# Expert weights: gate and up of most experts in one 4 MB transfer, in a ring of ten adjacent places

## The chip, the cores and the metric

The kernel runs on one core of a Trainium2 chip. Its time is the device time of one execution in microseconds, as the median of three runs. Two layers are computed, and each has an expert phase in which all 32 experts' weights are read from HBM, whatever the tokens are.

## What is computed

Two layers of a decoder with 512 tokens of width 1024, all in float32. A layer is a token mixer (a short gated convolution in layer 0, a chunked mLSTM in layer 1) beside a cross-attention into a memory, an output projection, a LayerNorm, a mixture of 32 experts, and a second LayerNorm. The change touches the experts alone:

```python
def expert_block(args):
    xblk, e = args
    h = jax.nn.silu(xblk @ w_gate[e]) * (xblk @ w_up[e])
    return h @ w_down[e]
```

`w_gate` and `w_up` are 1024 x 512, `w_down` is 512 x 1024 for each expert: three matrices of 2 MB. A token goes to two experts of one group of four, so that an expert has some 32 tokens.

## The kernel before

**The stream of weights.** The host packs the weights of a layer into `w_pack[l, e, 3, 128, 4096]`, a unit being `[128, 4096]` floats, 2 MB in one piece of HBM with 16 KB for each partition. Units 0 and 1 of an expert are gate and up together, each for half of the 1024 input rows (`("gu", e, 0)`, `("gu", e, 1)`); the third is down (`("dn", e, 0)`). `STREAM` (lines 42 to 45) lists a layer's 96 units in the order of their loads: both halves of expert 0, then for each expert e its two gate-and-up halves and the down unit of expert e - 1, and last the down unit of expert 31.

**The ring.** Ten places of 16 KB in each partition hold units: nine in the tensor `ring`, and the tenth, place 9, in the tensor `xT`, which stands behind `x_sb` (lines 96 to 99; `unit`, line 162). Unit n goes to place `PLACE[n % 10]` (line 50), so it takes the place of unit n - 10. The same memory serves the other phases: `R0`, `R1` and `R2` are thirds of the ring, and several split weights and activations of the mLSTM phase lie at fixed places of it.

**Who issues and who waits.** SP issues all loads, on one queue, in stream order. Units 0 to 9 are issued in the output projection ahead of the expert phase (`out_sp`, lines 702 to 717). Units 10 and 11 go in halves, each half when TensorE has read that half of the place (`half_read`, lines 1158 to 1162). Units 12 to 93 go whole: `unit_free(n - UNITS)` waits until TensorE is through with the old unit, then `load_unit` issues the transfer (lines 1163 to 1165). A gate-and-up unit is free at `gu_done`, a down unit at `y_done`. Units 94 and 95 go in two halves each (lines 1166 to 1171). In layer 0, loads for the mLSTM phase follow on the same queue, each behind `vacated(place)`.

TensorE waits for a unit with `unit_landed` (line 185), one semaphore for each place. For expert e it does the two halves of gate and up (`gate_up`, line 1235, matmuls at line 1244), the gather of later rows (line 1230), `combine` of expert e - 2 (line 1311), `down` of expert e - 1 (line 1282, matmuls at line 1294) and small transposes. `gate_up` asks for its two halves one after the other; `down` asks for its unit alone.

GpSimd gathers and scatters the tokens' rows through its own queue, 512 KB each, eight of each kind in a layer.

Of the kernel before, what the change touches and what calls it, by code (L numbers as in the profile page):

```python
# [4 lines left out]
F32 = mybir.dt.float32  # L5
# [8 lines left out]
P = 128  # L14
D_MODEL = 1024
SEQ = 512
DEPTH = 2
# [9 lines left out]
N_EXPERTS = 32  # L27
# [7 lines left out]
KT = D_MODEL // P  # L35
MT = MEM_LEN // P
BLK = 64
RING = 3
W_UNIT = 4096
W_EXP = 3 * W_UNIT  # L40
UNITS = 3 * RING + 1
STREAM = [("gu", 0, 0), ("gu", 0, 1)]
for _e in range(1, N_EXPERTS):
    STREAM += [("gu", _e, 0), ("gu", _e, 1), ("dn", _e - 1, 0)]
STREAM += [("dn", N_EXPERTS - 1, 0)]
SLOTS = 128
BIG = 1e30
SMALLS = 352
GATE_ROWS = 96 + ML_HEADS
PLACE = (0, 1, 2, 5, 4, 6, 8, 7, 3, 9)  # L50
EARLY = (0, 0)
HALVED = 2


class Chain:
# [16 lines left out]
def build_trunk(nc, x, xT_in, memT_in, conv_slabs, conv_qm, mlstm_w_in, smalls, w_kv_mem, w_out,  # L72
                ln1_g, ln1_b, ln2_g, ln2_b, w_pack, out):
    ctx = ExitStack()
    with ctx:
        phase_sems = []

        def sb(name, shape, dt=F32, at=ctx):
            return at.enter_context(nc.sbuf_tensor(name, shape, dt))

        def sem(name, at=ctx):
            if at is ctx:
                return ctx.enter_context(nc.semaphore(name))
            handle = nc.alloc_semaphore(name=name)
            phase_sems.append(handle)
            return handle
# [6 lines left out]


        ring_at = -(-nc.sbuf_base // 32) * 32
        ring = sb("ring", [P, RING * W_EXP])
        x_sb = sb("x_sb", [P, TT, D_MODEL])
        xT_at = -(-nc.sbuf_base // 32) * 32
        xT = sb("xT", [P, KT, SEQ])
        ident = sb("ident", [P, P])  # L100
        future_big = sb("future_big", [P, P])
        before = sb("before", [P, P], BF16)
# [52 lines left out]
        in_unit = [None] * DEPTH  # L155

        def place_of(kind, e, h=0):

            n = STREAM.index((kind, e, h))
            return PLACE[n % UNITS], n // UNITS  # L160

        def unit(i):
            if i == 3 * RING:
                return xT[:, :, :].rearrange("p k s -> p (k s)")
            return ring[:, i * W_UNIT:(i + 1) * W_UNIT]

        def gate_up_view(i):
            return unit(i).rearrange("p (c f x) -> p c f x", c=4, f=2)

        def down_view(i):  # L170
            return unit(i).rearrange("p (f c d) -> p f c d", f=2, c=2)

        def load_unit(eng, l, n):

            kind, e, h = STREAM[n]
            at = PLACE[n % UNITS]
            eng.dma_start(unit(at), w_pack[l, e, 2 if kind == "dn" else h]).then_inc(in_unit[l][at], 16)

        def load_half(eng, l, n, a):

            kind, e, h = STREAM[n]
            at, z = PLACE[n % UNITS], slice(W_UNIT // 2 * a, W_UNIT // 2 * (a + 1))
            eng.dma_start(unit(at)[:, z], w_pack[l, e, 2 if kind == "dn" else h][:, z]).then_inc(in_unit[l][at], 16)

        def unit_landed(eng, l, kind, e, h=0):

            i, use = place_of(kind, e, h)
            by_halves = use and i in PLACE[:HALVED]
            eng.wait_ge(in_unit[l][i], 16 * (use + (2 if by_halves else 1)))

# [884 lines left out]
        def load_mlstm_slab(sp, i):  # L1077
            c, w = slabs[i]
            sp.dma_start(R0[:, (i % 2) * 4096:(i % 2) * 4096 + KT * w], mlstm_w_in[:, KT * c:KT * (c + w)]
                         ).then_inc(in_w[i % 2], 16)  # L1080

        def expert_phase(l, mem_l):
# [3 lines left out]
            with ph:  # L1086
                s = lambda n: sem(f"{n}_{l}", ph)
# [26 lines left out]
                half_read = s("p2_half_read")  # L1114
                in_unit[l] = [s(f"in_unit_{i}") for i in range(UNITS)]
                back = [s(f"p3_back{t}") for t in range(TT)]
# [21 lines left out]
                with nc.Block() as block:  # L1138
                    @block.sync
                    def _(sp):  # L1140
                        def unit_free(n):

                            kind, e, h = STREAM[n]
                            if kind == "gu":
                                sp.wait_ge(gu_done, 2 * e + h + 1)
                            else:
                                sp.wait_ge(y_done, e + 1)

                        def vacated(place):

                            unit_free(max(n for n in range(len(STREAM)) if PLACE[n % UNITS] == place))

                        if l == 0:
                            conv_sp(sp)
                        out_sp(sp)
                        for row, dst in ((ln2_g, ln_g), (ln2_b, ln_b)):
                            sp.dma_start(dst[0:1, :], row[l].unsqueeze(0)).then_inc(in_ln, 16)
                        for n in range(UNITS, UNITS + HALVED):
                            sp.wait_ge(half_read, n - UNITS + 1)
                            load_half(sp, l, n, 0)  # L1160
                            unit_free(n - UNITS)
                            load_half(sp, l, n, 1)
                        for n in range(UNITS + HALVED, len(STREAM) - 2):
                            unit_free(n - UNITS)
                            load_unit(sp, l, n)
                        for i, e in enumerate((LAST - 1, LAST)):
                            at, _ = place_of("dn", e)
                            unit_free(len(STREAM) - 2 + i - UNITS)
                            for f, done in ((0, in_unit[l][at]), (1, last_dn[i])):
                                sp.dma_start(down_view(at)[:, f], w_pack[l, e, 2].rearrange("p (f c d) -> p f c d", f=2, c=2)[:, f]  # L1170
                                             ).then_inc(done, 16)
                        if not last_layer:
                            vacated(7)
                            sp.dma_start(wkv[:, 0], w_kv_mem[1].rearrange("p (h k n) -> p h k n", h=2, k=KT)[:, 0]
                                         ).then_inc(in_kv_half[0], 16)
                            sp.wait_ge(gu_done, 2 * N_EXPERTS)
                            sp.dma_start(memT, memT_in.rearrange("p (k m) -> p k m", k=KT)).then_inc(in_mem2, 16)
                            sp.dma_start(wkv[:, 1], w_kv_mem[1].rearrange("p (h k n) -> p h k n", h=2, k=KT)[:, 1]
                                         ).then_inc(in_kv_half[1], 16)
                            vacated(0)  # L1180
                            load_mlstm_slab(sp, 0)
                        later_sp(sp)
                        for i in range(3):
                            sp.wait_ge(scattered[i], 16 * len(range(i, N_GROUPS, 3)))
                        if not last_layer:
                            for t in range(TT):
                                sp.dma_start(x_sb[:, t, :], x2_dram[t * P:(t + 1) * P, :]).then_inc(back[t], 16)
                            vacated(1)
                            load_mlstm_slab(sp, 1)
# [29 lines left out]
                    def _(pe):  # L1219
# [15 lines left out]
                        def gate_up(e, halves=(0, 1)):  # L1235
                            if e >= 2:
                                pe.wait_ge(hid_done, e - 1)
                            for h in halves:
# [3 lines left out]
                                for c in range(4):  # L1242
                                    for f in range(2):
                                        last = nc.tensor.matmul(GU_BANK[e % 2][64 * f:64 * f + 64, :],  # L1244
                                                                xgT[e // 2 % 2][:, 4 * h + c, 64 * (e % 2):64 * (e % 2) + 64],
                                                                gu[:, c, f, :], start=(h == 0 and c == 0), stop=(h == 1 and c == 3))
                                    if c == 1 and 2 * e + h < HALVED:
                                        last.then_inc(half_read, 1)
# [327 lines left out]
        def later_blocks(l, ph, x1_rows, to_rows, ln_g, ln_b, scattered, acc_read):  # L1576
# [4 lines left out]
            s = lambda n: sem(f"later_{n}_{l}", ph)  # L1581
# [41 lines left out]
            def later_sp(sp):  # L1623
                def before():
                    for i in range(3):
                        sp.wait_ge(scattered[i], 16 * len(range(i, N_GROUPS, 3)))
                    for t in range(TT):
                        sp.dma_start(x_sb[:, t, :], x1_rows[t * P:(t + 1) * P, :]).then_inc(again, 16)

                def step(e, n, b):  # L1630
                    sp.wait_ge(y_done, n + 1)
                    for h, done in ((0, in_gu1), (1, in_gu1), (2, in_dn1)):
                        sp.dma_start(unit(3 + h), w_pack[l, bass.ds(e, 1), h].rearrange("o p x -> p (o x)")).then_inc(done, 16)

                def after():
                    for t in range(TT):
                        sp.wait_ge(normed, t + 1)
                        sp.dma_start(to_rows[t * P:(t + 1) * P, :], x_sb[:, t, :]).then_inc(put, 16)
                    sp.wait_ge(put, 16 * TT)
                turns(sp, step, before=before, after=after)  # L1640
# [906 lines left out]
```

## Time and profile before

| | us |
|---|---|
| median of three runs | 1393.65 (1392.25 to 1394.54) |
| span of the profiled execution | 1392.8 |
| TensorE busy in it | 1338.4 (96%) |
| layer 0, expert units from first issue to last half | 142 to 652 |
| layer 1, the same | 874 to 1378 |
| HBM read | 460 MB |

The profile is one execution, so its span stands beside the median of the runs and not for it. Times within it count from the span's start. Matmuls overlap, so that TensorE's busy share is high whether it waits or not. A DMA issue is known by the time at which SP issued it, and by the microseconds from there to its landing; the packets of a queue are counted with their bytes and the share of the 16 DMA engines' time that they took. "DMA share" in a stretch is that of all queues and can come out a little over 1, as packets overlap. The transfers to place 9 have the name `xT` and the others `ring`.

### The profile page before, as it was taken

To read this page: it belongs to the slowest core of one execution; us is meant where nothing else is said; L and a number is where in the kernel's file an instruction comes from. 1 tells how busy PE (TensorE), PEld (TensorE's weight loads), DVE (VectorE), ACT (ScalarE), POOL (GpSimd) and SP (SyncE) were. 2 spreads that over 40 slices of the span, in tenths; PEclk is the share of its full clock that TensorE was granted. 3 is DMA by queue.
4 is the path that set the end of the run, shared out by engine and by line. 5 is a ranking of instruction groups with operands and counts; after the bars stand their busy time and mean duration, and the time that the engine had idled before them with its cause. 6 is when DMAs were issued, how large, how long until landed. Compare 5 with 4: busy or idle time off the path is not lost. (4 is left out here: it accounts for less than half of the span.)

```text
span 1392.8 us, 16438 instructions
## 1 busy us (share of the span) xinstructions
PE 1338.4 (96%) x6694; PEld 711.7 (51%) x6694; DVE 509.8 (37%) x1038; ACT 306.1 (22%) x534; POOL 41.4 (3%) x66
## 2 busy tenths in 40 slices
PE   8999999999999999989899999999999999999896
PEld 7878783333333333333787788774333333333332
DVE  5366583122122121222554358782132122122122
ACT  5242341011011010111443236441011011010111
POOL 1000000000000000000000000000000000000000
PEclk9999999999999999999999999999999999999998
DMA  9420879999999999999431201989999999999995
GB/s 376 172 92 0 363 293 372 427 426 428 427 425 427 427 428 426 427 428 392 190 121 61 106 16 61 409 335 382 429 428 426 428 426 428 428 425 428 427 427 225
DMA packets 41395, 465.36 MB, mean 334 GB/s; under 512 B 6602, under 2 KB 6754, under 8 KB 13030
## 3 DMA queue, kind: packets, MB, share of 16 engines
q1 hardware_dynamic: 36422, 454.83, 78.4%
q0 software_dynamic: 4608, 8.40, 1.6%
q8 instruction: 55, 0.90, 0.3%
q10 hardware_dynamic: 288, 1.05, 0.2%
q14 instruction: 22, 0.18, 0.0%
HBM read 460.05 MB, written 12.60 MB: 339 GB/s over the span
## 5 line engine op out<-in xcount | busy, mean ns | idle before, releaser
L1244 PE MATMUL bank<-ring,kv_sb 128*64 128x512 f32 x960 | 214.7, 596 | 11.2 <-DMA ring<-in_w_pack 11.1
L1244 PE MATMUL bank<-ring,onehot 128*64 128x512 f32 x896 | 203.7, 603 | 13.4 <-DMA ring<-in_w_pack 13.4
L1294 PE MATMUL bank<-ring,pad 128*64 128x512 f32 x928 | 211.8, 598 | 1.8 <-issue 1.1
L1244 PEld LDWEIGHTS bank<-ring,kv_sb 128*64 128x64 f32 x960 | 68.4, 137 | 135.8 <-issue 135.5
L1294 PEld LDWEIGHTS bank<-ring,pad 128*64 128x64 f32 x928 | 61.8, 136 | 143.8 <-issue 135.0
L1244 PEld LDWEIGHTS bank<-ring,onehot 128*64 128x64 f32 x896 | 64.4, 138 | 131.7 <-issue 131.7
L1407 ACT ACTIVATE pad<-bank 128x256 f32<-128x256 f32 x64 | 24.5, 383 | 437.1 <-PE bank L1244 437.1
L1413 ACT COPY pad<-bank 128x512 f32<-128x512 f32 x64 | 37.4, 585 | 329.2 <-PE bank L1294 329.2
L1497 DVE COPY onehot<-bank 128x512 f32<-128x512 f32 x32 | 22.1, 691 | 237.0 <-PE bank L1230 237.0
L1507 DVE COPY pad<-bank 128x256 f32<-128x256 f32 x64 | 27.0, 422 | 173.5 <-PE bank L1269 173.5
L1497 DVE COPY kv_sb<-bank 128x512 f32<-128x512 f32 x28 | 19.4, 691 | 188.8 <-PE bank L1230 188.8
L1230 PEld LDWEIGHTS bank<-x_sb 128*128 128x128 f32 x480 | 58.1, 191 | 48.6 <-issue 47.1
L1311 PE MATMUL bank<-pad,x_sb 64*128 64x512 f32 x256 | 71.7, 639 | 0.0
L1230 PE MATMUL bank<-x_sb 128*128 128x128 f32 x480 | 69.5, 288 | 0.0
L497 PE MATMUL bank<-x_half_hi,w_half_hi 128*128 128x512 f32 x160 | 63.0, 394 | 1.5 <-DVE x_half_lo L577 1.1
L497 PE MATMUL bank<-x_half_lo,w_half_hi 128*128 128x512 f32 x160 | 62.3, 389 | 0.0
L497 PE MATMUL bank<-x_half_hi,w_half_lo 128*128 128x512 f32 x160 | 62.3, 389 | 0.0
L1975 PE MATMUL bank<-x_half_hi,w_half_hi 128*128 128x512 f32 x112 | 44.0, 393 | 0.0
L1975 PE MATMUL bank<-x_half_hi,w_half_lo 128*128 128x512 f32 x112 | 43.6, 390 | 0.0
L1975 PE MATMUL bank<-x_half_lo,w_half_hi 128*128 128x512 f32 x112 | 43.6, 389 | 0.0
L2106 DVE TENSOR_TENSOR w_half_lo<-ring,w_half_hi 128x1024 fp32r<-128x1024 f32 x24 | 29.5, 1239 | 37.5 <-ACT w_half_hi L2066 37.5
L1501 DVE TENSOR_TENSOR pad<-pad,bank 128x256 f32<-128x256 f32 x64 | 26.3, 410 | 30.0 <-ACT pad L1407 30.0
(345 smaller groups left out, 1723.4 us busy)
## 6 DMA issues: line engine op xcount, KB each, us to landing
ring<-in_w_pack SPq DMA_DIRECT2D x166, 2048.0 KB, 27.3
xT<-in_w_pack SPq DMA_DIRECT2D x18, 2048.0 KB, 30.1
ring<-in_w_pack SPq DMA_DIRECT2D x16, 1024.0 KB, 25.1
ring<-in_mlstm_w_in SPq DMA_DIRECT2D x6, 2048.0 KB, 8.4
ring<-in_conv_slabs SPq DMA_DIRECT2D x5, 1536.0 KB, 12.1
ring<-in_w_out SPq DMA_DIRECT2D x1, 4096.0 KB, 13.8
x_rows<-x_sb SPq DMA_DIRECT2D x6, 512.0 KB, 8.2
ring<-in_xT SPq DMA_DIRECT2D x4, 512.0 KB, 6.7
```

The costliest lines, as they stand in the source:

```text
L497: last = nc.tensor.matmul(o[:, :], w[:, k, :], xh[:, k, :], start=(k == 0 and w is w_hi and xh is x_hi), stop=(k == KT - 1 and w is w_lo))
L1230: last = nc.tensor.matmul(o[:, c * P:(c + 1) * P], xg[g % 3][:, 512 * h + c * P:512 * h + (c + 1) * P], pick[g % 2][:, 2 * (q % 2):2 * (q ...
L1244: last = nc.tensor.matmul(GU_BANK[e % 2][64 * f:64 * f + 64, :], xgT[e // 2 % 2][:, 4 * h + c, 64 * (e % 2):64 * (e % 2) + 64], gu[:, c, f ...
L1294: last = nc.tensor.matmul(Y_BANK[e % 2][64 * n:64 * n + 64, :], hidT[e % 2][:, c, 64 * f:64 * f + 64], dn[:, f, c, 512 * n:512 * n + 512], ...
L1311: last = nc.tensor.matmul(ACC[n][:, :], gateT[e // 2 % 2][rows, e % 2, :], y[e % 2][rows, :], start=(j == 0), stop=(j == PER_GROUP - 1))
L1407: nc.scalar.activation(hid[e % 2][:, :], GU_BANK[e % 2][:, 0:256], ACT.Silu).then_inc(activated, 1)
L1413: nc.scalar.copy(y[e % 2][:, :], Y_BANK[e % 2][:, :]).then_inc(y_copied, 1)
L1497: V.tensor_copy(xgT[q % 2][:, 4 * h:4 * h + 4, :], o[:, :].rearrange("p (c r) -> p c r", c=4)).then_inc(xcopied, 1)
L1501: V.tensor_tensor(hid[e % 2][:, :], hid[e % 2][:, :], GU_BANK[e % 2][:, 256:512], ALU.mult).then_inc(hid_done, 1)
L1507: V.tensor_copy(hidT[e % 2][:, :, :].rearrange("p c r -> p (c r)"), H_BANK[:, 0:256]).then_inc(hcopied, 1)
L1975: last = nc.tensor.matmul(o[:, :], w[:, k, :], xh[:, k, :], start=(k == 0 and w is hi and xh is x_hi), stop=(k == KT - 1 and w is lo))
L2106: last = V.tensor_tensor(of(lo), part, of(hi), ALU.subtract)
```

## The change

Ten places now lie in one tensor `ring`, place 9 behind place 8; `xT` is laid over place 9, and `x_sb` comes after. The first ten units keep their old places (`FIRST_PLACES`). Later units go round the ring in the order 0, 1, 2, 4, 5, 6, 7, 8, 9, 3 (`PLACES`), and each waits for the last unit that had its place, which is no longer always unit n - 10. `PAIRED` lists the first gate-and-up units from 14 on whose second half goes to the next place; expert 31 is left out. That gives 19 pairs in a layer: experts 5 to 9, 12, 14 to 19, 22 and 24 to 29. A pair is one transfer of 4 MB (`load_pair`), issued when both places are free, with one semaphore increment, and both of its halves wait for that (`landing`). The host packs the weights as `w_pack[l, e, 128, 3, 4096]`, so that a partition's three units lie one behind the other, 48 KB in all: a pair is a run of 32 KB for each partition, a single unit a run of 16 KB with 48 KB from one partition's to the next. Matmuls and their order stay.

```diff
-PLACE = (0, 1, 2, 5, 4, 6, 8, 7, 3, 9)
+FIRST_PLACES = (0, 1, 2, 5, 4, 6, 8, 7, 3, 9)
+PLACES = (0, 1, 2, 4, 5, 6, 7, 8, 9, 3)
+PLACE = FIRST_PLACES + PLACES * (-(-len(STREAM) // UNITS) - 1)
+PAIRED = [n for n in range(14, len(STREAM) - 4) if STREAM[n][0] == "gu" and STREAM[n][2] == 0 and PLACE[n + 1] == PLACE[n] + 1]
+
+
+def landing(n):
+
+    first = n - 1 if n - 1 in PAIRED else n
+    at = PLACE[first]
+    counts = [16 * (2 if UNITS <= m < UNITS + HALVED else 1) for m in range(first + 1) if PLACE[m] == at and m - 1 not in PAIRED]
+    return at, sum(counts)
...
-        ring = sb("ring", [P, RING * W_EXP])
+        ring = sb("ring", [P, UNITS * W_UNIT])
+        xT_at = ring_at + 4 * RING * W_EXP
+        xT = nc.alloc_sbuf_tensor_at("xT", [P, KT, SEQ], F32, offset=xT_at)
+        units = ring[:, :].rearrange("p (i x) -> p i x", x=W_UNIT)
         x_sb = sb("x_sb", [P, TT, D_MODEL])
-        xT_at = -(-nc.sbuf_base // 32) * 32
-        xT = sb("xT", [P, KT, SEQ])
...
-            at = PLACE[n % UNITS]
-            eng.dma_start(unit(at), w_pack[l, e, 2 if kind == "dn" else h]).then_inc(in_unit[l][at], 16)
+            at = PLACE[n]
+            eng.dma_start(unit(at), w_pack[l, e, :, 2 if kind == "dn" else h]).then_inc(in_unit[l][at], 16)
+
+        def load_pair(eng, l, n):
+
+            _, e, _ = STREAM[n]
+            at = PLACE[n]
+            eng.dma_start(units[:, at:at + 2, :], w_pack[l, e, :, 0:2]).then_inc(in_unit[l][at], 16)
...
-            i, use = place_of(kind, e, h)
-            by_halves = use and i in PLACE[:HALVED]
-            eng.wait_ge(in_unit[l][i], 16 * (use + (2 if by_halves else 1)))
+            at, count = landing(place_of(kind, e, h)[1])
+            eng.wait_ge(in_unit[l][at], count)
...
+                        def place_free(n):
+
+                            unit_free(max(m for m in range(n) if PLACE[m] == PLACE[n]))
...
                         for n in range(UNITS + HALVED, len(STREAM) - 2):
-                            unit_free(n - UNITS)
-                            load_unit(sp, l, n)
+                            if n - 1 in PAIRED:
+                                continue
+                            place_free(n)
+                            if n in PAIRED:
+                                place_free(n + 1)
+                                load_pair(sp, l, n)
+                            else:
+                                load_unit(sp, l, n)
...
-    pack = _np.empty((DEPTH, N_EXPERTS, 3, P, W_UNIT), _np.float32)
+    pack = _np.empty((DEPTH, N_EXPERTS, P, 3, W_UNIT), _np.float32)
```

## Rows read from the trace of the kernel before

**Rows 1.** The page, 40 slices: share of the DMA engines, rate.
```profile
DMA  9420879999999999999431201989999999999995
GB/s 376 172 92 0 363 293 372 427 426 428 427 425 427 427 428 426 427 428 392 190 121 61 106 16 61 409 335 382 429 428 426 428 426 428 428 425 428 427 427 225
```
**Rows 2.** Stretches of layer 1's expert phase: engines, clock, DMA share, GB/s.
```profile
936.00:991.00 55.00, 55.00 (x310) 21.33 (x310) 14.46 (x38) 7.53 (x14) 3.11 (x3) 0.97 0.97 390
...
1050.00:1200.00 150.00, 150.00 (x718) 55.15 (x716) 37.81 (x73) 19.61 (x32) 6.04 (x6) 1.00 1.01 427
```
**Rows 3.** Chain of waits, two experts' beginnings: start us, us, what.
```profile
991.00 7.02 PE bank L1244 x32
...
1004.12 7.02 PE bank L1244 x32
```
**Rows 4.** Chain of waits, the end of layer 1.
```profile
1215.42 43.36 DMA ring<-in_w_pack
...
1262.60 45.70 DMA ring<-in_w_pack
...
1317.86 44.86 DMA ring<-in_w_pack
```
**Rows 5.** Groups by line: busy, mean ns, then idle us before and releaser.
```profile
L1244 PE MATMUL bank<-ring,kv_sb 128*64 128x512 f32 x960 | 214.7, 596 | 11.2 <-DMA ring<-in_w_pack 11.1
...
L1244 PE MATMUL bank<-ring,onehot 128*64 128x512 f32 x896 | 203.7, 603 | 13.4 <-DMA ring<-in_w_pack 13.4
...
L1244 PE MATMUL bank<-xT,onehot 128*64 128x512 f32 x128 | 29.1, 596 | 2.5 <-DMA xT<-in_w_pack 2.5
```
**Rows 6.** Waits of SP's queue: us in total, times, longest.
```profile
SPq L177 <- PE bank L1244: 400.5, 110, 9.7
SPq L177 <- PE bank L1294: 287.1, 54, 6.3
```
**Rows 7.** SP's timeline, one issue each: start us, us of issuing.
```profile
241.26 0.33 SPq L177 DMA_DIRECT2D ring<-in_w_pack  x1
257.81 0.33 SPq L177 DMA_DIRECT2D xT<-in_w_pack  x1
...
958.09 0.33 SPq L177 DMA_DIRECT2D ring<-in_w_pack  x1
968.18 0.33 SPq L177 DMA_DIRECT2D ring<-in_w_pack  x1
977.34 0.33 SPq L177 DMA_DIRECT2D ring<-in_w_pack  x1
984.72 0.33 SPq L177 DMA_DIRECT2D xT<-in_w_pack  x1
994.63 0.33 SPq L177 DMA_DIRECT2D ring<-in_w_pack  x1
```
**Rows 8.** us to landing of those issued at 241.26, 257.81, 968.18, 984.72, 994.63; w_out.
```profile
ring<-in_w_pack SPq DMA_DIRECT2D x1, 2048.0 KB, 8.3
xT<-in_w_pack SPq DMA_DIRECT2D x1, 2048.0 KB, 12.0
ring<-in_w_pack SPq DMA_DIRECT2D x1, 2048.0 KB, 8.7
xT<-in_w_pack SPq DMA_DIRECT2D x1, 2048.0 KB, 11.8
ring<-in_w_pack SPq DMA_DIRECT2D x1, 2048.0 KB, 11.7
...
ring<-in_w_out SPq DMA_DIRECT2D x1, 4096.0 KB, 13.8
```
**Rows 9.** SP's queue from 56.61 to 63.87, then 276 to 299: packets, MB, share.
```profile
q1 hardware_dynamic: 95, 3.11, 99.2%
...
q1 hardware_dynamic: 677, 9.78, 100.1%
```
**Rows 10.** SP's queue from 779 to 784.5, an mLSTM slab landing: packets, MB, share.
```profile
q1 hardware_dynamic: 129, 1.82, 77.7%
```

## What the change should do to the time

> **What bounds the kernel now.** Both expert phases stream 96 units of 2 MB per layer, and the question is whether TensorE or the stream sets their end. I read the 40-slice view first [rows 1]: in both expert phases the DMA row stands at 9 and the GB/s row at 425 to 428 from a slice after the start to the end. The stretches [rows 2] say it more finely: in the first 55 us of layer 1's phase the 16 DMA engines are 0.97 busy at 390 GB/s, then 1.01 at 427, up to the end. So DMA idles only near the start of the phase, and from then on never. PE does one expert in 13.1 us (two beginnings of gate and up, 991.00 and 1004.12 [rows 3]); three units at 428 GB/s are 3 x 2.097 MB / 428 = 14.7 us. PE is the faster of the two by 1.6 us per expert, and it begins with a full ring of ten units (49 us of stream). That lead is used up after some 25 experts. The chain of waits [rows 4] ends so: its last 170 us hold three pieces "DMA ring<-in_w_pack" of 43 to 46 us, with some matmuls between them. A transfer that takes 44.9 us from issue to landing with 4.9 us of own work has nine others ahead of it: the queue is full and PE waits for it. By lines, gate and up lost 11.1 + 13.4 + 2.5 = 27.0 us to w_pack transfers in the two phases [rows 5]. So the time is: when the last unit lands, plus a tail that does not change. And the last unit lands when the first did, plus 4.9 us per unit, plus **every microsecond in which the DMA queue ran dry**. It can run dry only early, while PE frees places slowly and the ring is full; SP itself waits for PE 400.5 + 287.1 us before such transfers [rows 6], which costs nothing while older transfers are queued.
>
> **Part 1: what a pair waits for (the dear part).** A transfer is issued when its place is free; from the issue times I read when each place is freed. In the kernel before, unit n takes the place of unit n-10, so the issue time of unit n is the time at which unit n-10 was used up. After the change, the places of the first ten units keep the old order (0, 1, 2, 5, 4, 6, 8, 7, 3, 9) and the later ones run 0, 1, 2, 4, 5, 6, 7, 8, 9, 3. So unit 13 now needs the place of unit 4 (before: 3), the pair 14+15 those of 3 and 5, unit 16 that of 7 (before: 6), the pair 17+18 those of 6 and 9, unit 19 that of 8, the pair 20+21 those of 10 and 11. In layer 1 units 4, 5, 7, 9 and 11 are used up at 958.09, 968.18, 977.34, 984.72 and 994.63 [rows 7]. PE does not move in this stretch: it reads units that landed long ago.
> Two prices are needed. A 2 MB unit issued into an empty queue lands after 8.7 us (issued at 968.18) or 8.3 us (issued at 241.26) [rows 8]; 8.5 less its own 4.9 leaves 3.6 us of way. A 4 MB transfer into an empty queue thus takes 8.5 + 4.8 = 13.1 to 13.3 us; the one that the trace has, w_out, took 13.8 [rows 8]. I take 13.1 (it is nearest in kind) and keep 13.8 for the range. Behind other transfers a unit lands 4.9, a pair 9.7 us after the one ahead.
> Layer 1, landing by landing. Unit 13: issued at 958.09, where before unit 14 stood; 958.1 + 8.5 = 966.6. Pair 14+15: issued at 968.18, lands at 968.2 + 13.1 = 981.3 (unit 15 landed at 968.2 + 8.7 = 976.9 before). Unit 16: issued at 977.34, 981.3 + 4.9 = 986.2. Pair 17+18: issued at 984.72, 997.8. Unit 19: 1002.7, where before it landed at 984.72 + 11.8 = 996.5 [rows 8]. Pair 20+21: 1002.7 + 9.7 = 1012.4, where before unit 21 landed at 994.63 + 11.7 = 1006.3 [rows 8]. **The stream is 6.1 us late.** From here the queue does not run dry: the next pair could land alone 13.1 us after its issue, which follows 13.1 us behind the last pair's, and the queue ahead of it needs 14.6.
> Layer 0 with its own times [rows 7]: pair 14+15 issued at 241.26, lands at 254.4; unit 16 at 259.3; pair 17+18 issued at 257.81, lands at 270.9; unit 19 at 275.8, before 257.81 + 12.0 = 269.8 [rows 8]: 6.0 late, 5.8 after the pair 20+21.
>
> **Part 2: what 32 KB runs save.** 19 pairs per layer fit the condition (experts 5 to 9, 12, 14 to 19, 22, 24 to 29; the others fall on the steps from place 2 to 4, 9 to 3 or 3 to 0, and expert 31 is left out), 16 of them after unit 21. The trace has 32 KB packets in one place, w_out: 95 packets in a window of 7.26 us at a share of 99.2%, so 0.992 x 16 x 7.26 / 95 = 1.213 us each. For weights in 16 KB packets: 9.78 MB in a window of 23 us are 597 of them (the other 80 are four bytes each), 1.001 x 16 x 23 / 597 = 0.617 us [rows 9]. Two small ones 1.23, one large 1.213: 0.02 us per large packet, eight of them per engine and pair, 0.16 us. But the weights in that window shared the engines with a few packets of other queues and w_out did not, so I take 0.10 and get 16 x 0.10 = 1.6 us per layer. The bound below is 0 (two packets of 16 KB are sent after all), above 0.2. This is small because a queued transfer here shows no fixed cost that could be merged away.
> The Trainium skill says otherwise: "DMA: Bandwidth & Descriptors", section "Anatomy of one DMA", gives each DMA a fixed cost of about 2 us beside its bytes, and the section "Rules for kernel authors" asks for large transfers. As an estimate by that page, 38 transfers less would give 76 us; the trace disagrees for queued transfers, since 2 MB at 428 GB/s leave none of the 2 us.
>
> **Part 3: the HBM layout.** A unit was 2 MB in one piece; now a partition's three units lie together, so an unpaired unit is 128 runs of 16 KB at a pitch of 48 KB. The nearest row is the mLSTM slab: 16 KB runs at a pitch of 107 KB; in a window of 5.5 us 1.82 MB, or 111 packets, took 0.777 x 16 x 5.5 / 111 = 0.616 us each [rows 10], the price of the contiguous weights. I take 0; for the range 0.5% of the stream either way, 2 us per layer, since that row is of a queue with one transfer only.
>
> **Part 4: what lies on no path.** SP issues 19 transfers less per layer, while it waits for PE anyway [rows 6]. Late in the phase PE waits for a pair's second half before it starts the first: 4.9 us at expert 29, which it wins back over the unpaired experts 30 and 31: after the landing of pair 29 PE has three times 13.1 us [rows 3] and a tail of 2 us to do, some 41.3 us; the stream has eight units of 4.9 us and a half unit's matmuls of 1.8 us behind the last, some 41.1. So 0.2 us per layer, 0.4 in all. If that cover were gone the price would be up to 4.9 us per layer. Gathers and scatters share the engines with packets that are twice as long: eight turns of 0.6 us more, and their rows are wanted tens of us later. xT's move behind the ring changes no instruction. The last units before the mLSTM phase keep their places' order to within one unit.
>
> **Sum.** Layer 1: +6.1 - 1.6 + 0.2 = +4.7. Layer 0: +5.8 - 1.6 + 0.2 = +4.4. Both carry to the end one for one, since the stream sets both ends. +9.1 us. The profiled execution (span 1392.8) would become 1401.9; the median of the runs is 0.85 above that span, so 1393.65 + 9.1 = **1402.7 us**.
>
> **The rivals.** (a) *The two runs are not merged* into one packet, or 32 KB packets cost the same per byte: Part 2 gives 0, the delay stands: 1393.65 + 6.1 + 5.8 + 0.4 = 1406. For it: only w_out shows such packets. Against: it does show them. (b) *The 48 KB pitch costs* in the full stream: 1% of some 390 us per layer is 3.9, 1402.7 + 7.8 = 1410. Against: rows 10. (c) *Not slower: the full stream runs faster*, by larger packets or by another spread over HBM. The price to beat is 4.5 us in 75 units, 0.06 us of 4.9 per unit, in paired and unpaired ones alike; it decides from 433 GB/s where rows 2 have 427, and gives 1394 there. Only the pairs have a reason for it, and at 1.213 us per packet they reach 432; gathers and scatters, which take the rest, stay. (d) *Each transfer has a fixed cost that the merge saves*: were it of the size of the way, 3.6 us for each of 38 transfers, the stream would stop being the bound, and PE's 27.0 us of waits are all that there is to win, 1367. Against: rows 9, where queued transfers keep the engines at 100.1%. (The Trainium skill's section on the fixed cost, named in Part 2, stands for this rival.)
>
> **How the numbers follow.** Forecast 0.68 (1399.5 to 1405.5: savings of 0 to 0.2 per pair, ways of 13.1 to 13.8); (a) 0.08; (b) 0.10; (c) 0.10, of which 0.08 ends within 0.2% (2.8 us, about what a measurement can tell) and 0.02 faster; (d) 0.04. Slower 0.86, same 0.08, faster 0.06. The range goes from 1397.5, the forecast with 0.5% less for the layout, to 1408, which holds (a) and the lower half of (b).
>
> **What would show it.** In the profile after: GB/s in the first 55 us of each expert phase below 390 and the DMA share below 0.97; the issue of unit 13 at 958, of the pairs at 968 and 985; after that a rate of 428 to 430; more than 27.0 us of PE's waits for w_pack, nearer 37, and beginning some four experts earlier; the mLSTM phase some 4 us later. The forecast is wrong if the share early in the phase is not lower, or if the full stream runs above 433 or below 425 GB/s.

## The result and the profile after

The changed kernel takes 1408.53 us as the median of four runs (1406.30 to 1409.45), beside 1394.10 us for the kernel before in the same session. The ratio on record, which is not the quotient of these two medians (1.0103), is 1.0101, with a 95% interval of 1.0085 to 1.0116. That is 14.1 us slower, between 11.9 and 16.2. A second session with the same kernel gave 1.0091 (1.0075 to 1.0108), 12.7 us. The forecast was 1402.7 us, with a range up to 1408.0: the direction was right, the size was not.

The profiled execution has a span of 1407.0 us. Four views of it answer rows of before.

First the page's 40 slices, as [rows 1]. What is new stands where an expert phase begins, in slices 7 and 28 to 29: 335, and 353 and 394 GB/s, where before it was 372, and 382 and 429.

```profile
DMA  9420978999999999998431202989999999999994
GB/s 374 169 91 0 379 293 335 407 424 434 427 425 435 422 429 431 428 428 360 188 120 61 105 16 78 407 333 353 394 428 433 424 433 430 422 430 430 427 428 199
```

Then stretches, as [rows 2]: us, busy time of PE, PEld, DVE, ACT and POOL, granted share of the clock, DMA share, GB/s. The first 55 us of layer 0's and of layer 1's expert phase, the same stretch of the full stream as before, and 17 us at the start of the mLSTM phase; then, from the kernel before, the 55 us of layer 0 that [rows 2] lack.

```profile
209.40:264.40 55.00, 55.00 (x316) 21.57 (x317) 15.12 (x40) 7.66 (x14) 3.20 (x3) 1.00 0.90 352
943.60:998.60 55.00, 55.00 (x316) 21.54 (x316) 15.29 (x40) 7.64 (x14) 3.12 (x3) 1.00 0.90 347
...
1050.00:1200.00 150.00, 145.53 (x692) 54.39 (x691) 37.56 (x73) 19.23 (x31) 5.03 (x5) 1.00 1.01 429
674.00:691.00 17.00, 13.12 (x95) 10.97 (x94) 7.78 (x10) 8.05 (x12) 2.26 (x4) 0.90 0.58 228
```

```profile
209.00:264.00 55.00, 55.00 (x309) 21.35 (x307) 14.62 (x38) 7.58 (x14) 3.33 (x3) 0.97 0.97 392
```

Where the DMA share was 0.97 before it is 0.90 now, in both layers; afterwards the engines are full as before, and this stretch runs at 429 GB/s in place of 427. So the loss is dry time at the start, as forecast; what the full stream gained is read from its landings below.

SP's issues at the start of layer 1, as [rows 7]: unit 13, the pair 14+15, unit 16, the pair 17+18 and unit 19; below, in the same order, the sizes and us to landing, as [rows 8].

```profile
965.75 0.33 SPq L187 DMA_DIRECT2D ring<-in_w_pack  x1
974.26 0.33 SPq L193 DMA_DIRECT2D ring<-in_w_pack  x1
983.37 0.33 SPq L187 DMA_DIRECT2D ring<-in_w_pack  x1
990.80 0.33 SPq L193 DMA_DIRECT2D ring<-in_w_pack  x1
991.17 0.43 SPq L187 DMA_DIRECT2D ring<-in_w_pack  x1
```

```profile
ring<-in_w_pack SPq DMA_DIRECT2D x1, 2048.0 KB, 7.5
ring<-in_w_pack SPq DMA_DIRECT2D x1, 4096.0 KB, 13.4
ring<-in_w_pack SPq DMA_DIRECT2D x1, 2048.0 KB, 9.4
ring<-in_w_pack SPq DMA_DIRECT2D x1, 4096.0 KB, 14.8
ring<-in_w_pack SPq DMA_DIRECT2D x1, 2048.0 KB, 19.3
```

The transfers wait for what the prediction named: unit 19 lands at 991.2 + 19.3 = 1010.5. Layer 1's stream began 7.6 us later than before (its first load was issued at 881.9, not 874.3), so that 1010.5 - 7.6 - 996.5 = 6.4 us were lost since. In layer 0, with no such shift, the pair 20+21 lands at 266.5 + 18.9 = 285.4, and unit 21 did at 279.6: 5.8 us.

The chain of waits at its end, as [rows 4] (start us, us, what):

```profile
1119.63 37.24 DMA ring<-in_w_pack
...
1160.74 40.43 DMA ring<-in_w_pack
...
1205.03 40.81 DMA ring<-in_w_pack
...
1312.65 38.87 DMA ring<-in_w_pack
```

and the two groups of gate and up, as [rows 5]:

```profile
L1269 PE MATMUL bank<-ring,onehot 128*64 128x512 f32 x1024 | 234.0, 610 | 17.1 <-DMA ring<-in_w_pack 17.1
...
L1269 PE MATMUL bank<-ring,kv_sb 128*64 128x512 f32 x1024 | 231.6, 605 | 17.2 <-DMA ring<-in_w_pack 17.2
```

TensorE waits 34.3 us for weights, not 27.0, and the chain's first transfer now stands at 1120 us instead of 1215. The later part of the phase is set by the stream more than before.

The 14.2 us between the two profiled executions split by milestones, each an issue or a landing of the traces, so:

| stretch | layer 0 | layer 1 |
|---|---|---|
| up to the landing of unit 9 | -0.2 | -0.1 |
| unit 9 to unit 21 landed | +6.0 (66.1 to 72.0) | +6.4 (66.7 to 73.1) |
| unit 21 to the last half landed | -0.8 (371.7 to 370.9) | -0.1 (371.2 to 371.1) |
| last landing to layer 1's first issue, or to the end | +2.6 (222.9 to 225.6) | +0.3 |

### The profile page after: what moved, and what is told of

Read it like the earlier page. It is cut to its first block and busy times, and to the rows that moved or that the text cites. A ratio compares the mean times of both kernels' runs of the same rounds, so it can differ in the third digit from the quotient of the medians.

```text
span 1407.0 us, 16438 instructions
## 1 busy us (share of the span) xinstructions
PE 1344.2 (96%) x6694; PEld 718.1 (51%) x6694; DVE 510.0 (36%) x1038; ACT 306.3 (22%) x534; POOL 41.2 (3%) x66
## 5 line engine op out<-in xcount | busy, mean ns | idle before, releaser
L1269 PE MATMUL bank<-ring,onehot 128*64 128x512 f32 x1024 | 234.0, 610 | 17.1 <-DMA ring<-in_w_pack 17.1
L1269 PE MATMUL bank<-ring,kv_sb 128*64 128x512 f32 x1024 | 231.6, 605 | 17.2 <-DMA ring<-in_w_pack 17.2
L1319 PE MATMUL bank<-ring,pad 128*64 128x512 f32 x1024 | 233.7, 598 | 1.1 <-issue 1.1
L1269 PEld LDWEIGHTS bank<-ring,kv_sb 128*64 128x64 f32 x1024 | 76.6, 139 | 149.8 <-issue 149.5
L1269 PEld LDWEIGHTS bank<-ring,onehot 128*64 128x64 f32 x1024 | 75.4, 140 | 152.0 <-issue 152.0
L1319 PEld LDWEIGHTS bank<-ring,pad 128*64 128x64 f32 x1024 | 68.4, 136 | 157.5 <-issue 156.1
L512 PEld LDWEIGHTS bank<-x_half_hi,w_half_hi 128*128 128x128 f32 x160 | 30.0, 188 | 10.7 <-DVE w_half_lo L581 2.0
```

The costliest lines, as they stand in the source:

```text
L512: last = nc.tensor.matmul(o[:, :], w[:, k, :], xh[:, k, :], start=(k == 0 and w is w_hi and xh is x_hi), stop=(k == KT - 1 and w is w_lo))
L1319: last = nc.tensor.matmul(Y_BANK[e % 2][64 * n:64 * n + 64, :], hidT[e % 2][:, c, 64 * f:64 * f + 64], dn[:, f, c, 512 * n:512 * n + 512], ...
```

## The experiments

The theory, called the queue theory in the expectations, is that of the forecast: the time is the dry time of the DMA queue at the start of each phase, less a little for each pair. Its rivals were that the pairs cost something of their own, that the layout in HBM does, and that the late pairs lower TensorE's clock at a price. Ratios are against the kernel before in the same session, and the us beside them are the ratio's. "First 55 us" are the 55 us that begin 2.2 to 2.4 us before SP issues unit 10, as in [rows 2] and in the stretches above. A mean clock is the granted share of the clock over the span, as the median of a kernel's runs.

**The order of places without pairs.**

```diff
-PAIRED = [n for n in range(14, len(STREAM) - 4) if STREAM[n][0] == "gu" and STREAM[n][2] == 0 and PLACE[n + 1] == PLACE[n] + 1]
+PAIRED = []
```

> The changed kernel without pairs: the new order of places and the new layout of the weights stay, every unit is a transfer of its own. Queue theory (the time is the dry time of the DMA queue early in the phase): unit 13 still waits for the down unit of expert 0 and unit 18 for the second half of expert 3, so the order alone costs about 4.3 us per layer, 8.7 in all: 1394.1 + 8.7 = 1402.8, with the DMA share of the first 55 us between before and after. Rival (what costs is that a pair waits for two places): without pairs the time falls back to 1394. If the pairs also lower the clock late in the phases, the mean granted clock here is 0.995 as before, not 0.987.

1.0045 (1.0031 to 1.0059), +6.3 us, between 4.3 and 8.2, where 8.7 were expected; median 1401.77. The rival falls: with no pair at all more than a third of the loss remains. It lies at the start of the phases:

```profile
209.10:264.10 55.00, 55.00 (x317) 21.59 (x317) 15.14 (x40) 7.69 (x14) 3.19 (x3) 1.00 0.93 370
937.30:992.30 55.00, 55.00 (x316) 21.48 (x316) 15.21 (x40) 7.58 (x14) 3.12 (x3) 1.00 0.93 371
```

The price per layer was put a little too high (4.3; the interval reaches to 4.1). Unit 9 to 21 took 69.9 and 68.6 us. The mean clock was 0.994 to 0.995, as without the change.

**Pairs only where the queue is full.**

```diff
-PLACE = FIRST_PLACES + PLACES * (-(-len(STREAM) // UNITS) - 1)
-PAIRED = [n for n in range(14, len(STREAM) - 4) if ...]
+PLACE = FIRST_PLACES * 4 + PLACES * (-(-len(STREAM) // UNITS) - 4)
+PAIRED = [n for n in range(40, len(STREAM) - 4) if ...]
```

> The changed kernel with the old order of places for the first 40 units and the new one, with 13 pairs per layer, from unit 40 on, where four transfers are queued. Queue theory: no dry time early, 13 pairs save 0.10 us each: 1.25 per layer, 1394.1 - 2.5 = 1391.6. Clock theory (late pairs make TensorE stand still longer, the granted clock falls to half in stretches, one of them at the start of the mLSTM phase): 2 to 3 us on top, 1394, and a mean clock below 0.99. Rival (pairs cost something of their own in the full queue): 1397 or more.

0.9998 (0.9987 to 1.0008), no difference: between -1.8 and +1.1 us. The loss is gone, with 13 pairs per layer in place, so pairs in a full queue have no price that this run shows; but the 2.5 us that they should save are not there either. The mean clock was 0.988. In the profile layer 1's first 55 us are not dry (in layer 0 they have 387 GB/s at 0.97):

```profile
934.60:989.60 55.00, 55.00 (x316) 21.50 (x316) 15.25 (x40) 7.63 (x14) 3.12 (x3) 1.00 0.99 399
```

**The layout in HBM alone**, on the kernel before:

```diff
-            eng.dma_start(unit(at), w_pack[l, e, 2 if kind == "dn" else h]).then_inc(in_unit[l][at], 16)
+            eng.dma_start(unit(at), w_pack[l, e, :, 2 if kind == "dn" else h]).then_inc(in_unit[l][at], 16)
...
-    pack = _np.empty((DEPTH, N_EXPERTS, 3, P, W_UNIT), _np.float32)
+    pack = _np.empty((DEPTH, N_EXPERTS, P, 3, W_UNIT), _np.float32)
```

> The kernel before with the new layout of the weights in HBM alone (a partition's three units one behind the other, 16 KB runs at a pitch of 48 KB). If the layout costs nothing, 1394.1 within 1 us and 16 KB packets of 0.615 us on average in the full stream; if it is what is missing in the forecast (5 us), 1399, and packets of 0.62 us or more.

1.0000 (0.9991 to 1.0010), median 1396.00 beside 1394.64. From unit 21 to the last half it takes 371.5 and 371.1 us, before 371.7 and 371.2, and its 16 KB packets in the full stream take 0.615 us on average. A pitch of 48 KB has no cost clear of the noise, which is 1.4 us.

**Pairs up to expert 19.**

```diff
-PAIRED = [n for n in range(14, len(STREAM) - 4) if ...]
+PAIRED = [n for n in range(14, 60) if ...]
```

> The changed kernel with pairs up to expert 19 alone (12 per layer instead of 19). Queue theory: the early dry time stays, 7 savings of 0.10 us per layer are lost: 1408.5 + 1.4 = 1409.9. Clock theory: without late pairs TensorE's waits are short as before, no half clock late in the phases and at the start of the mLSTM phase, 2 to 3 us less than that: about 1407, with a mean clock of 0.993 or more.

1.0085 (1.0071 to 1.0100), +11.9 us, between 9.9 and 13.9; median 1408.32 beside 1394.64. By the ratio 1409.9 lies too high and 1407 within, while the median itself lies between the two: whether the late half clock has a price, this run does not tell. The mean clock returned to 0.995, so the half clock late in the phases comes with the late pairs. Unit 9 to 21 took 76.2 and 75.7 us, with 336 and 338 GB/s in the first 55 us at a clock of 0.97.

**Waiting for both halves, without pairs**, on the kernel before:

```diff
                             for h in halves:
                                 pe.wait_ge(xcopied, h + 1 if e == 0 else 2 * (e // 2) + 2)
+                                if h == 0 and 12 <= e < LAST - 1:
+                                    unit_landed(pe, l, "gu", e, 1)
                                 unit_landed(pe, l, "gu", e, h)
```

> The kernel before, in which TensorE waits for both halves of gate and up before it begins the first one, for experts 12 to 29; transfers, places and layout are those of before. Queue theory: the stream does not change, TensorE wins the 4.9 us of a bunched wait back over experts 30 and 31: 1394.6 + 0.4 = 1395.0. Clock theory (the bunched waits lower the granted clock): mean clock 0.991 or less, half clock in stretches after 460 and after 1220 us, as in the changed kernel; if these have a price of their own, 2 to 3 us more, 1397.5.

0.9991 (0.9982 to 1.0000), median 1393.49. The bunched waits of Part 4 cost nothing that can be measured. The clock was 0.992 on average over the runs (0.990 to 0.994), lower than before's 0.995, but not as low as with late pairs: bunched waits are at most a part of what lowers it.

**The changed kernel once more.** No edit.

> The changed kernel once more, for a second profile. Queue theory: from the landing of unit 9 to that of unit 21 it takes 72 to 76 us per layer, against 66 to 67 before, whatever the clock does; 1408.5. If the half clock at the start of the mLSTM phase belongs to the change, the time from layer 0's last landing to layer 1's first issue is again 225 us or more, and not 222 to 223.

1.0091 (1.0075 to 1.0108), median 1406.76. This profiled execution was the fastest of its six runs, with a span of 1402.2 us. Unit 9 to 21 took 75.3 and 70.9 us, the second a little below the 72 to 76 expected. The time from layer 0's last landing to layer 1's first issue was 222.2 us, as before: the extra 2.6 us at the start of the mLSTM phase do not come with the change each time. The first two stretches are the starts of the phases, the third the 17 us that lost clock in the first profile (0.90 there, 1.00 here):

```profile
208.20:263.20 55.00, 55.00 (x309) 21.43 (x307) 14.46 (x38) 7.47 (x14) 3.19 (x3) 0.97 0.87 339
940.80:995.80 55.00, 55.00 (x316) 21.52 (x316) 15.28 (x40) 7.62 (x14) 3.08 (x3) 1.00 0.90 354
...
674.00:691.00 17.00, 14.75 (x110) 12.25 (x109) 10.15 (x14) 7.87 (x12) 2.27 (x4) 1.00 0.74 291
```

**Pairs in the middle alone.**

```diff
+PLACE = FIRST_PLACES * 3 + PLACES * (-(-len(STREAM) // UNITS) - 3)
+PAIRED = [n for n in range(30, 68) if ...]
```

> The changed kernel with the old order of places for the first 30 units and 8 pairs per layer, from unit 35 to 66: the queue is full at the first of them, and the last lie before TensorE begins to wait for the stream. Queue theory: 0.10 us saved per pair, 0.8 per layer: 1394.6 - 1.6 = 1393.0, mean clock 0.995 as before. If pairs cost something in a full queue, 1395 or more; if late pairs alone do, less than e2_late_pairs had (1394.75).

0.9998 (0.9987 to 1.0009). Again no difference; the 1.6 us that 16 pairs should have saved lie within the interval, so this run neither shows nor excludes them. The mean clock, 0.990, was lower than expected although the last pair is that of unit 65.

**The same waits, two transfers instead of one.** Units of a pair are issued one behind the other when both places are free.

```diff
-                            if n in PAIRED:
+                            if n in TOGETHER:
                                 place_free(n + 1)
-                                load_pair(sp, l, n)
-                            else:
-                                load_unit(sp, l, n)
+                            load_unit(sp, l, n)
```

(`TOGETHER` is the changed kernel's `PAIRED`, and `PAIRED` is empty.)

> The changed kernel, in which each pair is issued as two transfers of 2 MB, one behind the other, when both places are free: its waits and places stay, the merged transfer goes. Queue theory as forecast: the early dry time stays at about 6 us per layer, since two units on an empty queue land 8.5 + 4.9 = 13.4 us after the issue, and the saving of the runs is lost: 1394.7 + 12.6 = 1407.3. If the excess over the forecast is the way of a 4 MB transfer on an empty queue (the second pair took 13.5 to 15.5 us in the profiles so far), the pair 17+18 lands 13.4 us after its issue here, and unit 9 to 21 takes 72.5 us or less per layer. Rival (the merge itself costs): the time falls to 1400 or less.

1.0095 (1.0078 to 1.0111), +13.3 us where 12.6 were expected, median 1408.44. With no merged transfer the loss is the same within the noise. So the waits for places are the loss, and the merge is not. SP's two issues for units 17 and 18 at 990.54, which landed after 10.3 us as the mean of the two, the first after 7.5 and so the second after 13.1:

```profile
990.54 0.80 SPq L188 DMA_DIRECT2D ring<-in_w_pack  x2
...
ring<-in_w_pack SPq DMA_DIRECT2D x2, 2048.0 KB, 10.3
```

The second was issued 0.37 us behind the first, so from the first issue to the last landing it took 13.5 us, and 13.3 in layer 0. The same pair merged took 12.9 and 14.8 in the profile after, and 12.9 to 15.5 (14.5 on average) in the six phases of the three profiles that have it: some 1 us more, which the whole times do not show. Unit 9 to 21 took 71.6 and 72.9 us, and unit 21 to the end 371.7 and 371.9, without the saving. The starts of the phases:

```profile
208.40:263.40 55.00, 55.00 (x309) 21.37 (x307) 14.44 (x38) 7.48 (x14) 3.20 (x3) 0.97 0.87 339
941.70:996.70 55.00, 55.00 (x308) 21.25 (x306) 14.53 (x38) 7.53 (x14) 3.13 (x3) 0.97 0.88 343
```

**All pairs but the first two.**

```diff
-PAIRED = [n for n in range(14, len(STREAM) - 4) if ...]
+PAIRED = [n for n in range(20, len(STREAM) - 4) if ...]
```

> The changed kernel without its first two pairs (units 14+15 and 17+18 go one by one), 17 pairs per layer stay. Queue theory: the early loss is that of the order of places alone, as in e1_order_only (2.7 us per layer in its profile), less 0.05 to 0.1 us for each of 17 pairs: 1394.7 + 2 x (2.7 - 1.3) = 1397.5, up to 1400 by the landing-by-landing sum. Rival (later pairs cost as much as the first two): 1406 or more.

1.0032 (1.0022 to 1.0042), +4.5 us, between 3.1 and 5.9; median 1399.97, at the upper of the two times expected. Two pairs per layer of 19 carry some two thirds of the loss in the measured times: with them it is 12.7 to 14.1 us. The rival falls. The starts of the phases:

```profile
209.10:264.10 55.00, 55.00 (x309) 21.39 (x307) 14.44 (x38) 7.47 (x14) 3.19 (x3) 0.97 0.90 359
939.10:994.10 55.00, 55.00 (x309) 21.34 (x309) 14.37 (x39) 7.53 (x14) 3.25 (x3) 0.97 0.91 361
```

**The old order for one round more.**

```diff
-PLACE = FIRST_PLACES + PLACES * (-(-len(STREAM) // UNITS) - 1)
-PAIRED = [n for n in range(14, len(STREAM) - 4) if ...]
+PLACE = FIRST_PLACES * 2 + PLACES * (-(-len(STREAM) // UNITS) - 2)
+PAIRED = [n for n in range(20, len(STREAM) - 4) if ...]
```

> The changed kernel with the old order of places for the first 20 units, and 17 pairs per layer from unit 20 on. Queue theory: nothing of the first round is left to wait longer; the pair 20+21 meets a queue of little depth: +0.4 us per layer, 1394.7 + 0.7 = 1395.4, unit 9 to 21 in 67 us per layer. Rival (pairs or the adjacent ring cost something besides the first ten replacements): 1399 or more.

1.0002 (0.9993 to 1.0012), median 1395.14. With 17 pairs per layer in the adjacent ring the loss is gone from the measured time, when the first ten replacements alone keep the old order. What the change costs in that time comes with units 10 to 19. The starts of the phases are again those of before:

```profile
209.20:264.20 55.00, 55.00 (x309) 21.37 (x307) 14.45 (x38) 7.52 (x14) 3.19 (x3) 0.97 0.97 388
939.20:994.20 55.00, 55.00 (x310) 21.27 (x308) 14.45 (x38) 7.47 (x14) 3.12 (x3) 0.97 0.97 386
```

Behind them this profile has a loss of its own: unit 9 to 21 took 69.9 and 70.2 us, not the 67 expected. The pair 20+21 waits for the place of unit 11 and landed 12.3 and 10.9 us behind unit 19, where units 20 and 21 took 9.8 before. The next 20 us have 373 and 394 GB/s, before 426 and 428, which is 2.5 and 1.6 us of stream. The execution took 1399.16 us, the longest of twelve and 4.0 above their median; how much of this a usual execution has, no trace shows.

No variant was clearly faster than the kernel before; the nearest is the wait for both halves, at 0.9991 with an interval that ends at 1.0000.

## Why the prediction was right or wrong

**What bounds the kernel: right.** The same stretches in all profiles put the loss where the DMA queue ran dry, and nowhere else of the same size.

**Part 1, what a pair waits for: right in its mechanism and nearly in its size.** It said 5.8 and 6.1 us per layer; the first profile has 6.0 and 6.4. Some of that closeness is luck: the issue times came from an execution with 3.4 us at half clock early in each phase, the first profile had none there, so that the pairs were issued 1.2 to 1.5 us earlier than forecast, and in layer 1 the second pair took 1.7 us longer. A fairer size comes from GB/s at the same clock, since the start of a phase has in some executions 3.4 us at half clock, 1.2 instead of 2.4 GHz (0.97 in the rows), and in others none (1.00). At 0.97 the old order of places has 392 and 390 before, 388 and 386 in the last experiment, 389 on average, the changed waits 339 [the second profile], 339 and 343 [two transfers], 340 on average. That is 49 x 55 / 428 = 6.3 us of stream per layer. At 1.00: 399 [pairs where the queue is full, layer 1] against 352, 347 and 354, 351 on average, 6.2 us. The profiles whose rows are not shown fit: 387 to 389 at 0.97 and 395 to 401 at 1.00 with the old order. The order alone is 399 less 370.5 at 1.00, 3.7 us, and the kernel without the first two pairs gives the same at 0.97 (389 less 360); the prediction did not split it off, and the expectation of the first experiment put it at 4.3. The other 2.5 us are the first two pairs, 5 in both layers; the measured times give them 8 to 10, and this difference stays open.
One price in it was too low for the second pair: 13.1 us for 4 MB on an empty queue. The first pair took 12.4 to 13.4 us in the three profiles that have it, the second one, which finds the end of unit 16 still on the way, 12.9 to 15.5. I had kept w_out's 13.8 as the upper bound; four of these six lie beyond it.
The 8.5 us for 2 MB were misread in one point: the queue was not empty at these issues. The transfer ahead of the one issued at 968.18 landed at 969.95, that of 241.26 at 242.99. Where the one ahead had landed, 2 MB took 7.3 to 8.6 us at the start of these phases.

**Part 2, what the runs save: the step that failed.** It took 0.10 us per pair, 1.6 per layer after unit 21. The packets themselves did that: 32 KB packets took 1.218 us on average in the full stream and 16 KB packets 0.615, so 0.012 us less per large packet, 0.10 per pair. But the landings followed only in part. From unit 21 to the last half the changed kernel took 370.9, 371.1, 369.9 and 370.6 us in its two profiles, on average 370.7; the two kernels with the old layout of transfers, before and the wait for both halves, and the one with the layout alone took 371.7, 371.2, 371.6, 371.1, 371.5 and 371.1, on average 371.4. That is 0.7 per layer where 1.6 stood. The other profiles scatter around this: without merged transfers 371.6 to 371.9 (the order alone, two transfers), without the first two pairs 370.6 and 370.8, with the second round in the old order 371.9 and 369.4. With 13, 8 and 17 pairs and no early loss three kernels had ratios of 0.9998, 0.9998 and 1.0002; the first and the last exclude 0.10 us per pair (2.6 and 3.4 us in all, against at most 1.8 and 1.0). In the last the price of the pair 20+21 may hide a saving. Where the other half of the packets' saving went was not settled. The bound below, 0, held.
The Trainium skill's fixed cost of a DMA ("DMA: Bandwidth & Descriptors", "Anatomy of one DMA") of about 2 us, which the page fitted to DMAs issued by GpSimd, is not seen here either: the last experiment has 34 transfers of SP's queue fewer and gave 1.0002, which is +0.3 us, between -1.0 and +1.7.

**Part 3, the layout: right** within the noise, 1.0000 with the layout alone.

**Part 4: right for the tail** (+0.3 us in the first profile, and no loss from bunched waits), **and wrong in what it left out**: late pairs lower the granted clock, 0.987 over the span where before it is 0.995. In the first profile one stretch of 3.4 us at half clock falls at 681 us, in the mLSTM phase, where TensorE is busy in all of the 3.4 us and the stream no longer full (a DMA share of 0.58 in the 17 us above). The transition took 2.6 us longer there, and not in the second profile, where that stretch kept its clock. 3.4 us at half clock can take 1.7 us of TensorE's work, so they explain the 2.6 at most in part. That a clock lowered late in the stream has a price in the time is not shown: three kernels with 0.988 to 0.990 are as fast as before.

**The sum.** With 6.25 us of loss and 0.7 of saving per layer it becomes 2 x 5.55 = 11.1, and 11.4 with the tail's 0.3. Of the 2.3 us above the forecast, 1.8 are Part 2's and 0.6 Part 1's. The measured ratios are 14.1 (11.9 to 16.2) and 12.7 us (10.5 to 15.1). The forecast's 9.1 lies outside both intervals; 11.4 lies within the second and just below the first. The same account gives 7.4 for the order alone (measured 4.3 to 8.2), 7.4 - 1.5 = 5.9 without the first two pairs (3.1 to 5.9, at its end), 12.5 for two transfers (10.9 to 15.5), 11.7 with pairs up to expert 19 (9.9 to 13.9) and, if the pair 20+21 is free, -1.5 with the second round in the old order (-1.0 to 1.7, so that this pair has a price or the saving is smaller). What is left of the changed kernel's own, 1 to 3 us, stays open: the transition held that much in one of two profiles.

**The range** ended at 1408.0 and the median of the first session was 1408.5. It had room for one dear term at a time. The way of a pair on an empty queue and the saving of the runs both came out on the dear side, and the start's half clock, there in one execution and not in another, was not in it. Its lower end is not what its reason gives: 1402.7 less 2 us for each layer is 1398.7, not 1397.5. One more sum is off, without consequence: a lead of 49 us at 1.6 per expert lasts for some 31 experts, not 25.

**Signs.** The DMA share early in the phase, the rate of 428 to 430 and the longer waits of TensorE came as listed (34.3 us, not nearer 37). Of layer 1's issues, less its shift of 7.6 us, unit 13's came at 958 as listed and the pairs' at 967 and 983, 1.5 us early; the waits began earlier than said, and layer 1 started 7.6 us later, not some 4.

## What to carry to other kernels

A transfer that is merged or moved waits for the last of the places it needs. Read from the issue times when each place comes free, and go landing by landing through the stretch where the queue is short: ten replacements decided this change, and 17 of 19 pairs in each layer had in the measured time neither cost nor gain. Where queued transfers already kept the engines busy, as here, fewer and larger ones won next to nothing; look for dry time instead. If a ring must be laid out anew, switch its order where several transfers are queued.

## What the runs showed of the hardware that was not expected

- **TensorE's clock reaches the stream.** The first 55 us of a phase have 3.4 us at half clock in some executions of the same kernel and none in others. With the old order of places that is 386 to 392 against 395 to 401 GB/s, with the changed waits 336 to 343 against 347 to 354: about 10 x 55 / 428 = 1.3 us of stream. The places come free later: in layer 0 of the changed kernel's two profiles unit 13 was issued 19.8 us after unit 10 without that stretch and 21.5 with it.
- **Late pairs and the clock.** Kernels with merged pairs after expert 19 had mean clocks of 0.987 to 0.990, kernels without any late pair and with the old waits 0.994 to 0.995; the same waits for places with two transfers per pair, 0.995. In the first profile TensorE had stretches of 3.4 to 6.8 us at half clock around 466, 510, 558, 1244 and 1292 us, in the part of the phases where it waits for weights. Bunched waits without merged transfers gave 0.992, so the cause is only half shown.
- **The first packets of a transfer on a short queue are slow.** In the changed kernel 9 to 15 of the first 16 packets of each of the first two pairs took 1.6 to 2.8 us, where those in a full queue take 1.2; and in the second pair of layer 1 the last two packets began at 1003.7 and 1004.0 us, 1 to 2 us behind the last ones of most other engines. On a queue that was empty, or whose last transfer landed within some 3 us, 4 MB took 12.4 to 15.5 us to land, 2 MB 7.3 to 9.1.
